# The output projection of a hybrid encoder layer as seven Strassen products

## The reference

```python
merged = g_a * branch_a + g_b * branch_b
x = x + merged @ w_out[i].astype(h.dtype)
```

## Time and profile before

| | |
|---|---|
| median of 3 runs | 1353.73 us (1353.56 to 1354.33) |
| the profiled execution: its own time | 1355.16 us |
| its span in the profile | 1353.4 us |
| TensorE busy | 1336.9 us, 99% |
| VectorE, ScalarE, GpSimd busy | 823.3, 610.6, 598.1 us |
| granted TensorE clock | 0.999 of full speed |
| from the first output matmul (1260.25) to the end of the span | 93.15 us |

### The profile page before, as it was taken

How to read it: one execution, slowest core, us unless ns; L and a number is a source line. 1 busy time by engine, 2 the same in 40 slices (tenths; PEclk the granted TensorE clock), 3 DMA queues, 4 the chain that set the end, 5 groups by cost and what they waited for, 6 DMA issues and landing times.

```text
span 1353.4 us, 20439 instructions
## 1 busy us (share of the span) xinstructions
PE 1336.9 (99%) x7056; PEld 1071.7 (79%) x7056; DVE 823.3 (61%) x985; ACT 610.6 (45%) x1157; POOL 598.1 (44%) x358
## 2 busy tenths in 40 slices
PE   7999999999999999999999999999999999999999
PEld 6878777888888888778788788787868878788787
DVE  6857777766776423667667576676665553578411
ACT  7564444554454333536445365364655443332200
POOL 3534644554454454343334333332357666444320
PEclk9999999999999999999999999999999999999999
DMA  7433654434333322766656647666565366434331
GB/s 214 177 81 117 171 150 124 162 109 124 93 109 109 124 93 93 278 215 200 217 186 206 216 153 225 219 195 218 208 242 187 127 209 211 151 135 179 138 109 62
DMA packets 123133, 221.16 MB, mean 163 GB/s; under 512 B 7713, under 2 KB 84257, under 8 KB 119762
## 3 DMA queue, kind: packets, MB, share of 16 engines
q1 hardware_dynamic: 58114, 172.12, 38.3%
q10 hardware_dynamic: 64880, 48.37, 11.2%
q0 software_dynamic: 96, 0.13, 0.0%
HBM read 152.05 MB, written 63.31 MB: 159 GB/s over the span
## 4 chain that ended last, share of the span: by engine, by line
PE 93%; DVE 4%; ACT 2%; issue 1%; DMA 0%; ACTq 0%; POOL 0%; DVEq 0%; POOLq 0%
PE F L199 38%; PE F L1059 35%; PE M L2012 3%; PE F L2012 3%; PE M L1262 2%; PE M L1306 2%; PE F L1276 1%; PE F L1300 1%; PE F L1293 1%; PE M L1300 1%; PE M L1293 1%; PE M L1255 1%; PE M L1287 1%; PE F L1964 1%; PE M L1011 0%
## 5 line engine op out<-in xcount | busy, mean ns | idle before, releaser
L1059 PE MATMUL F<-sb_tv,sb_whl 128*128 128x512 f32 x1200 | 287.9, 395 | 0.0
L199 PE MATMUL F<-sb_xb,sb_whl 128*128 128x512 f32 x1152 | 282.9, 402 | 0.0
L1059 PEld LDWEIGHTS F<-sb_tv,sb_whl 128*128 128x128 f32 x1200 | 224.9, 187 | 55.1
L199 PE MATMUL F<-sb_X,sb_whl 128*128 128x512 f32 x1104 | 259.6, 397 | 0.0
L199 PEld LDWEIGHTS F<-sb_xb,sb_whl 128*128 128x128 f32 x1152 | 214.1, 188 | 57.0 <-issue 8.1
L199 PEld LDWEIGHTS F<-sb_X,sb_whl 128*128 128x128 f32 x1104 | 207.9, 188 | 51.4 <-ACT sb_whl L208 0.2
L211 POOL TENSOR_TENSOR sb_whl<-sb_wst,sb_whl 128x1024 fp32r<-128x1024 f32 x56 | 139.1, 2485 | 242.9 <-ACT sb_whl L208 242.4
L470 POOL TENSOR_TENSOR sb_whl<-sb_acc,sb_whl 128x512 fp32r<-128x512 f32 x123 | 171.7, 1404 | 159.9 <-ACT sb_whl L527 159.9
L1059 PE MATMUL F<-sb_xb,sb_whl 128*128 128x512 f32 x900 | 219.4, 396 | 0.6 <-POOL sb_whl L470 0.6
L1059 PEld LDWEIGHTS F<-sb_xb,sb_whl 128*128 128x128 f32 x900 | 168.1, 187 | 45.4 <-issue 2.5
L527 ACT ACTIVATE sb_whl<-sb_acc 128x512 fp32r<-128x512 f32 x123 | 76.0, 627 | 98.7 <-PE F L1059 87.3
(11 more groups left out here) (225 smaller groups left out, 1796.3 us busy)
## 6 DMA issues: line engine op xcount, KB each, us to landing
sb_wst<-w_units SPq DMA_DIRECT2D x56, 512.0 KB, 4.4
sb_acc<-cs_d SPq DMA_DIRECT2D x8, 2048.0 KB, 7.1
sb_wst<-w_units SPq DMA_DIRECT2D x14, 1024.0 KB, 4.9
sb_acc<-w_units SPq DMA_DIRECT2D x12, 1024.0 KB, 5.1
x_d<-sb_res ACTq DMA_DIRECT2D x24, 512.0 KB, 3.2
sb_early<-x_d SPq DMA_DIRECT2D x8, 1024.0 KB, 5.9
sb_acc<-ecs_d SPq DMA_DIRECT2D x16, 512.0 KB, 8.3
g_d<-sb_res ACTq DMA_DIRECT2D x16, 512.0 KB, 5.7
```

The lines of the kernel that those rows point to most:

```text
L199: last = nc.tensor.matmul(bank, weight(slot, wp, k), act(ap, k, half), start=(k == 0 and wp == 0 and ap == 0), stop=(k == NK - 1 and wp == 1))
L1059: last = nc.tensor.matmul(F[:, BANK[what], :], ring(idx, wp)[:, k * P:(k + 1) * P], moving(what, ap, k), start=(idx < 4 and k == 0 and wp ...
```

## The change

`merged` is cut in four blocks of 512 rows (time) by 512 contraction channels, A11, A12, A21, A22 (`merged_block(r, c)`), `w_out` in B11 to B22, and the product is made by the Winograd form of Strassen's scheme: seven products of 512 x 512 x 512 in place of eight.

- TensorE (`out_product`): P0 = A11 B11, then A12 B21 added onto it, and five more, in the order left operand A11, A12, S3, S2, S1, A22, S4. Each product is 4 contraction tiles x 4 row blocks x 3 matmuls = 48, in four banks (M is `X_BANKS`, F is `Y_BANKS`); seven make 336. Each takes two units of weights, so a unit (slot n % 2) now feeds 24 matmuls.
- VectorE, after the merge, works a list of 88 operations: 16 block sums of 128 x 512 (`sums`), their 16 low parts (`sum_lows`), four sums of weight blocks of two 128 x 1024 operations each (`operand_sum`), twelve low parts of weights of 128 x 1024 (`operand_low`), four + four that carry sums of products (u2, u3), twelve additions of x to such sums (`with_rows`), and sixteen that read a product's bank and finish an output block. That is 68 operations of 128 x 512 and 20 of 128 x 1024.
- ScalarE: 16 high parts of sums (`sum_high`), twelve of weights (two by `high`, ten by `operand_high`), and four copies of P0 out of PSUM before A12 B21 is added to it (`p1_copied`).
- GpSimd: its last six low parts fall away; after the last turn of the merge it has nothing.
- SyncE: the eight loads of x rows between merge turns fall away. After the merge it issues two single units, four blocks of two units (`load_block`, 1 MB each: R12, R22, R11, R21, into the space of X1 that the merge's matmuls have read) and four blocks of x rows (`load_rows`, 1 MB each); then the 16 stores as before, in the order of the finished blocks.
- The merge: tiles 0 to 3 keep only their first half's split (A21, their second half, is used only in sums), so four high parts and four low parts of 128 x 512 fall away there.

```diff
+            def sum_high(n):
+                for k in range(4):
+                    act.wait_ge(sum_done, sum_base + 4 * S_ORDER.index(n) + k + 1)
+                    nc.scalar.activation(sum_split(n, 0, k), sum_block(n)[:, k, :], ACT.Copy).then_inc(x_hi, 1)
+            def operand_high(n):
...
+                act.wait_ge(unit_done, 2 * (OUT + n - 1))
+                nc.scalar.activation(weights(n % 2, 0), operand_raw(n), ACT.Copy).then_inc(w_hi, 1)
...
+                            if h and not second:
+                                continue
...
+            operand_low(2)
+            sums(1)
+            sums(3)
+            operand_low(3)
...
+            operand_sum(R12, R22, R12, ALU.subtract)
+            dve.wait_ge(sum_done, sum_base + 8)
+            sum_lows(3)
+            operand_low(4)
+            sums(2)
...
+            operand_sum(R11, R12, R11, ALU.add)
+            operand_low(5)
+            sum_lows(2, (0, 1))
+            dve.wait_ge(rows_in, 16)
+            for t in range(4):
+                finished(1, t)
+                nc.vector.tensor_tensor(rows11[:, t, :], rows11[:, t, :], X_BANKS[:, t, :], ALU.add).then_inc(out_ready, 1)
+            operand_low(6)
+            sum_lows(2, (2, 3))
+            sums(4)
+            operand_low(7)
+            sum_lows(1)
...
+            operand_sum(R12, R22, R11, ALU.subtract)
+            operand_low(8)
+            for t in range(4):
+                finished(3, t)
+                dve.wait_ge(p1_copied, pair_base + t + 1)
+                nc.vector.tensor_tensor(u2_rows[:, t, :], u2_rows[:, t, :], X_BANKS[:, t, :], ALU.add).then_inc(u2_done, 1)
+            for t in range(4):
+                dve.wait_ge(u2_done, pair_base + t + 1)
+                nc.vector.tensor_tensor(u3_rows[:, t, :], u2_rows[:, t, :], Y_BANKS[:, t, :], ALU.add).then_inc(u3_done, 1)
+            operand_low(9)
...
+            with_product(4, 5, rows21, Y_BANKS, ALU.subtract)
+            with_product(8, 6, rows12, X_BANKS, ALU.add)
...
+            def out_product(idx, banks, adds, left, left_ready, freed):
+                for k in range(4):
+                    n = 2 * idx + k // 2
+                    if k % 2 == 0:
+                        pe.wait_ge(w_hi, OUT + n + 1)
...
+            out_product(0, X_BANKS, False, merged_left(0, 0), merged_ready(0, 0), None)
+            out_product(1, X_BANKS, True, merged_left(0, 1), merged_ready(0, 1), (p1_copied, pair_base))
...
+            out_product(2, Y_BANKS, False, sum_left(3), sum_ready(3), None)
+            out_product(3, X_BANKS, False, sum_left(2), sum_ready(2), (out_ready, 0))
+            out_product(4, X_BANKS, False, sum_left(1), sum_ready(1), (u2_done, pair_base))
+            out_product(5, Y_BANKS, False, merged_left(1, 1), merged_ready(1, 1), (u3_done, pair_base))
+            out_product(6, X_BANKS, True, sum_left(4), sum_ready(4), (out_ready, 4))
```

More of the change, by code:

```diff
@@ L1772, in _, with load_block, load_rows, store @@
                 for s in range(2):
-                    sp.wait_ge(m_lo, i * 4 + (2 * s + 2))
+                    sp.wait_ge(acc_ready, i * 4 + (2 * s + 2))
                     load_merge(i + 1, s)
                     load_w(sp, B3 + 20 + s, 2, i)
[L1776 to L1788, removed]
+            def load_block(b, to, c, kh):
+                at = PLAIN + NT + OUT + 4 * c + 2 * kh
+                sp.dma_start(to.rearrange("p (a c) -> p a c", a=2), a["w_units"][at:at + 2].rearrange("a p c -> p a c")).then_inc(block_in[b][0], 16)
+            def load_rows(to, r, c, sem=rows_in):
+                sp.dma_start(to, a["x"][r * HALF:(r + 1) * HALF, c * HALF:(c + 1) * HALF].rearrange("(t p) c -> p t c", p=P)).then_inc(sem, 16)
+            load_w(sp, OUT + 2, 0, 0)
+            sp.wait_ge(unit_done, 2 * OUT)
+            load_block(0, R12, 1, 0)
+            load_block(2, R22, 1, 1)
+            load_w(sp, OUT + 3, 0, 0)
+            load_block(1, R11, 0, 0)
+            sp.wait_ge(acc_ready, 16)
+            load_rows(rows11, 0, 0)
+            load_block(3, R21, 0, 1)
+            sp.wait_ge(x_lo, s_count(1, 3))
+            load_rows(rows22, 1, 1, rows22_in)
+            sp.wait_ge(x_lo, s_count(4, 3))
+            load_rows(rows21, 1, 0)
+            load_rows(rows12, 0, 1)
+            def store(count, r, c):
+                for t in range(4):
+                    sp.wait_ge(out_ready, count + t + 1)
+                    from_ = (rows11, rows12, rows21, rows22)[2 * r + c][:, t, :]
+                    at = (4 * r + t) * P
+                    sp.dma_start(out[at:at + P, c * HALF:(c + 1) * HALF], from_).then_inc(out_stored, 16)
+            store(0, 0, 0)
+            store(4, 1, 1)
+            store(8, 1, 0)
+            store(12, 0, 1)
             sp.wait_ge(out_stored, 16 * 2 * NT)
@@ L1822, in _ @@
             low(pool, B3 + 19, 2, 3)
-            with nc.gpsimd.Fori(0, 3) as i:
-                for s in range(2):
-                    low(pool, B3 + 26 + s, 2, i)
         @block.scalar
@@ L1916, in _ @@
             nc.vector.reciprocal(ms, ms).then_inc(rms_ready, 1)
[L1917 to L1931, removed]
@@ new lines, in with_product @@
+            def with_product(at, idx, rows_, banks, op):
+                for t in range(4):
+                    dve.wait_ge(rows_added, pair_base + at + t + 1)
+                    finished(idx, t)
+                    nc.vector.tensor_tensor(rows_[:, t, :], rows_[:, t, :], banks[:, t, :], op).then_inc(out_ready, 1)
+            operand_low(2)
+            sums(1)
+            sums(3)
+            operand_low(3)
+            dve.wait_ge(block_in[0][0], block_in[0][1] + 16)
+            dve.wait_ge(block_in[2][0], block_in[2][1] + 16)
@@ new lines, in _ @@
+            for t in range(4):
+                dve.wait_ge(u2_done, pair_base + t + 1)
+                nc.vector.tensor_tensor(u3_rows[:, t, :], u2_rows[:, t, :], Y_BANKS[:, t, :], ALU.add).then_inc(u3_done, 1)
+            operand_low(9)
+            dve.wait_ge(block_in[3][0], block_in[3][1] + 16)
+            operand_sum(R21, R11, R21, ALU.subtract)
+            operand_low(10)
+            sum_lows(4)
+            dve.wait_ge(rows22_in, 32)
+            with_rows(rows22, u3_rows, u3_done)
@@ L1994, in _ @@
                     unit3(18 + s, X1, i)
[L1996 to L2017, removed]
@@ new lines, in out_product @@
+            def out_product(idx, banks, adds, left, left_ready, freed):
+                for k in range(4):
+                    n = 2 * idx + k // 2
+                    if k % 2 == 0:
+                        pe.wait_ge(w_hi, OUT + n + 1)
+                        if n < 2:
+                            pe.wait_ge(w_lo, OUT + n + 1)
+                        else:
+                            pe.wait_ge(t_lo2, low_base + n - 1)
+                    left_ready(k)
+                    for t in range(4):
+                        if k == 0 and freed:
+                            pe.wait_ge(freed[0], freed[1] + t + 1)
+                        for wp, ap in ((0, 0), (1, 0), (0, 1)):
+                            last = nc.tensor.matmul(banks[:, t, :], left(ap, k)[:, t * P:(t + 1) * P],
+                                                    weights(n % 2, wp)[:, (k % 2) * HALF:(k % 2 + 1) * HALF],
+                                                    start=(not adds and k == 0 and wp == 0 and ap == 0), stop=(k == 3 and ap == 1),
+                                                    skip_group_check=adds)
+                        if k == 3 and t < 3:
+                            last.then_inc(row_done, 1)
+                    if k % 2:
+                        last.then_inc(unit_done, 2)
```

152 lines of the change are left out of this document (128 added, 24 removed).

## The result

| | median | range, runs | ratio to before, 95% interval |
|---|---|---|---|
| before, beside it | 1353.99 us | 1353.56 to 1354.33, 4 | |
| changed | 1342.17 us | 1342.05 to 1342.74, 4 | 0.9914 [0.9897, 0.9931] |
| before, a second time | 1353.67 us | 1353.11 to 1355.34, 9 | |
| changed, a second time | 1342.13 us | 1341.94 to 1342.80, 5 | 0.9913 [0.9900, 0.9927] |

What follows compares the result with a forecast made beforehand. The prediction took the output stage to be bound by TensorE alone: 48 fewer matmuls at 0.2333 us take 11.2 us off with no stall, from the median of 1353.73 us to 1342.5 us, range 1341.9 to 1346.3.

Steps and rivals of the forecast that it cites:

- The sum: Output stage: 48 fewer matmuls at 0.2333 us take 11.2 us off, with no stall; 1342.5 us.
- VectorE's steps: VectorE's output-stage list: small operations 0.61 us apart, large 1.13, so 64.1 us of work in 72.3 of room.
- rival 1: VectorE's step is its whole length, 0.69 and 1.22 us, making its list late; 1343.9 us, chance 0.12.
- The merge's tail: Merge's end: VectorE catches up 4.6 us, so P0's second unit's low part stands at 1264.0, spare 1.9 us.
- rival 2: VectorE does not catch up in the merge, P0's middle waits 1.7 us; 1344.2 us, chance 0.10.
- The late rows: Last x rows, issued at 1315.6, land by 1324.2 before unit 12's low part; spare 1.3 to 3 us.
- rival 3: Late x rows at 163 GB/s land by 1331, 5.5 us of stall; halfway 2 to 3 us, 1345; chance 0.14.
- the wait for rows in front of unit 12's low part at zero: Sign expected in the profile after: VectorE has zero wait for x rows ahead of unit 12's low part.
- rival 4: VectorE becomes the bound at steps of 0.81 and 1.64 us, list 87.9 us; slower, 1357.8 us, chance 0.04.
- The least spare: VectorE's tightest due time in the output stage: unit 9, middle of P4, spare 1.2 us; P4's bank 1.3.
- beyond it the loss is one for one: Late x rows: past the spare of 1.3 to 3 us, each microsecond of delay costs one microsecond.

Runs made afterwards that it cites:

- e7_before_336: Kernel before without the last of the output stage's eight contraction tiles, 336 matmuls instead of 384; 1342.27 us, ratio 0.9917.
- e4_extra4: Changed kernel with four extra VectorE additions in front of the sums into u2, each waiting for the one before; 1343.08 us, ratio 0.9921.
- e1_all_splits: Changed kernel with the unused splits of the second halves of tiles 0 to 3 kept in the merge; 1344.51 us, ratio 0.9941.
- e5_rows_late: Changed kernel with two useless 1 MB loads issued in front of the last two blocks of x rows; 1346.23 us, ratio 0.9941.
- e8: Changed kernel with twelve useless 128 x 1024 additions on GpSimd, one behind each high part of weights; 1350.67 us, ratio 0.9977.
- e3: Changed kernel with block sums S2 and S4 moved ahead of the low part of unit 3, nothing added; 1346.47 us, ratio 0.9949.
- e4_extra8: Changed kernel with eight extra VectorE additions in front of the sums into u2, each waiting for the one before; 1348.36 us, ratio 0.9958.
- e2_gpsimd_lows: Changed kernel with the twelve low parts of weights on GpSimd instead of VectorE; 1347.54 us, ratio 0.9956.

## Why the prediction was right

- **The sum.** 48 matmuls at the step of the chain, 11.2 us, nothing back. e7_before_336 shows it by itself (11.2), the chain of the changed kernel has 11.20 for each product. The stage's other 0.2 us are two small differences: 0.1 from first matmul to last addition (78.66 us for 336, 89.96 for 384, so 11.30) and 0.07 in the tail, 3.12 for 3.19. The remainder to 11.8 lies in the runs of before: of the 33 beside the experiments 20 took 1353.03 to 1353.82 and 13 took 1354.07 to 1355.34, and a median of few runs falls between. The lowest runs, 1353.03 and 1341.94, are 11.1 apart. The fall at 993 us costs 1.7, so it would fit 1355.34 and the profiled 1355.16, but not the other twelve, which lie about 1.0 above the lower ones; what lifts those stays open.
- **VectorE's steps, rival 1.** It fell. 0.62 and 1.13 hold over 72 us of list, and the times forecast with them were met to 0.2 us or better at units 3, 5 and 9 and u2. So the rule of the Trainium skill ("VectorE: DVE Perf Modes", The DRAIN you can't avoid) doesn't decide here; its exemption for operations that are not held does. How near it was to counting is shown by e4_extra4: 2.9 us more, and P4 waits.
- **The merge's tail, rival 2.** It fell, and the mechanism is shown by its removal: with the change VectorE stands idle for 0.27 us ahead of the merge's last half, waiting for its matmuls, where it came 4.6 us late before, and e1_all_splits brings the late unit back, at 2.1 us. The forecast had 1.7, since in before the low part ended at 1267.6. The last L211 ended at 1263.22, and 1264.0 less 1.13, 1262.9, was forecast:

```profile
1260.52 2.70 POOL L211 TENSOR_TENSOR sb_whl<-sb_wst,sb_whl 128x1024 fp32r<-128x1024 f32 x1 [5.64 <-ACT sb_whl L208]
```

- **The late rows, rival 3.** They came in time, but one of the signs that I named was wrong, "the wait for rows in front of unit 12's low part at zero". The row of the changed kernel:

```profile
1323.39 1.23 DVE L2058 TENSOR_TENSOR sb_whl<-sb_early,sb_whl 128x1024 fp32r<-128x1024 f32 x1 [2.96 <-DMA sb_acc<-x]
```

  VectorE waits 2.96 us. It follows from the prediction's own numbers: rows at 1324.2 (1323.1 in this profile), VectorE free of the four L2071 that began at 1317.96, thus by 1320.4. A wait was sure; only its end counted. It ended 0.3 later than forecast, the low part at 1324.62, and P6 began at 1326.3 with 1.7 to spare. The landing itself was the term with an error in it: 1315.6, 5.6 and 2.5 make 1323.7 and not the 1324.2 written, and 1315.6 + 6.3 make 1321.9 and not 1322.5. The rows landed 8.9 us after S4's low parts (1314.50 to 1323.4), where 5.6 + 2.5 are 8.1; the 0.5 written too much hid most of that. e5_rows_late shows the other side of that spare.
- **VectorE as the bound, rival 4.** Not there: the list ran from 1266.07 to 1338.5 with TensorE. Even with eight meetings with GpSimd (e8), 64.1 + 13.5 = 77.6 us of list, the kernel stayed below before, as the 83.8 of the rival's threshold says. That no meeting remains was the condition, and the groups by form of the changed kernel show none above its undisturbed length.
- **The least spare.** Forecast at unit 9 (1.2) and P4's bank (1.3); measured 1309.5 - 1308.33 = 1.2 and 1303.9 - 1302.7 = 1.2. For delays ahead of u2 it is 2.0, by the 0.82 of idle time in front, which the prediction didn't count.
- **What was mis-sized:** the cost of a late VectorE, in all that I wrote of rivals and of e3, e4_extra8 and e5: "beyond it the loss is one for one". That held for five waits of 0.6 to 1.1 us and for one of 2.07; behind one of 1.93 and behind those of 2.34 and more the clock fell and 1.5 to 2.8 us came on top, as the last section lists. The forecast itself didn't use the term, since the changed kernel has no wait.

## What to carry to other kernels

Price a product taken away by the step of the matmuls in the chain, not by their length, and then go through the list of the engine that takes over the work against the due time of every buffer: here 64 us of work fit in 72, and the order alone was worth 4.3 (the median; 2.7 in the fastest execution). Leave a spare at each due time and measure it with two, four and eight useless operations, since here a wait of about 2 to 4 us mostly cost 1.5 to 2.8 more than its length. An idle GpSimd is no free help for a nearly full VectorE: twelve operations moved to it cost 5.4 us here, where VectorE did them for nothing, and twelve useless ones beside it 8.5.

## What the hardware showed beyond that

**A wait of TensorE costs its length, and then often the clock.** Waits in the stage, and what the product or half product behind them took more than without a wait. Each row is one profiled execution. The wait is counted from the end of the matmul before, which stands 0.16 us behind the step (48 matmuls read 11.36 us long and follow one another at 11.20), so the next product starts the wait and 0.16 late:

| kernel | wait, us | lowest clock behind it | more, us |
|---|---|---|---|
| e8_gpsimd_idle_work, four waits | 0.59 to 1.08 | 1.00 | 0.1 each |
| e4_extra4 | 0.76 | 1.00 | 0.1 |
| e8_gpsimd_idle_work, ahead of P2 | 1.93 | 0.50 | 1.8 |
| e1_all_splits | 2.07 | 1.00 | 0.1 |
| e3_sums_first | 2.34 | 0.50 | 1.6 |
| e5_rows_late | 2.70 | 0.50 | 1.5 |
| e2_gpsimd_lows | 3.17 | 0.50 | 1.6 |
| e4_extra8 | 3.67 | 0.50 | 2.8 |

0.50 is the lower of the two levels, 1.2 GHz. The Trainium skill ("TensorE: Matmul & The Clock Gate", What's actually happening) says that the clock has these two levels and none between; the stretches inside a fall read 0.50 and those outside 1.00, and a value such as 0.70 over 5 us is a mean of both. The length of the wait alone doesn't decide: the clock fell behind 1.93 us in e8 and not behind 2.07 in e1, and in before at 993 us it fell behind shorter gaps, several in a row. What else decides these runs don't show.

**VectorE against GpSimd.** A meeting costs VectorE 1.7 us (4.18 for 2.49), and in e8 no group that reads PSUM was slowed (675 ns at L2109). The Trainium skill ("GPSIMD Engine Reference", Key points) puts the contention on VectorE's instructions with two SBUF inputs, and the trace agrees: L2037, L2043 and L2062 have two, L2109 has one. GpSimd in its turn had a mean of 2846 ns for an addition that took 1.89 us beside a group that reads PSUM.
